# Memory attention in head pairs, a moved transpose group in the first mixer, and head sums by token quarters in the second

## The chip, the cores and the metric

The program runs on one core of one Trainium2 chip. The metric is the device time of one execution in microseconds; lower is better. The figure of a kernel is the median of its runs.

The core's engines run side by side and meet through semaphores: TensorE (PE in the profile; PEld is its weight load), VectorE (DVE), ScalarE (ACT), GpSimd (POOL) and SyncE (SP), which issues the DMAs of the weights.

## The reference, cut to what matters

The sequence has 256 tokens of width 1024, in float32. A first block has two layers; each is a mixer, an attention over 256 memory rows with four heads, an output product, and a SwiGLU network. The mixer of layer 0 is a sparse attention, that of layer 1 an RWKV-7 recurrence. A second block (a gated MLP, a forgetting attention and another SwiGLU network) follows. The change touches the mixers and their memory attention:

```
def _mem_attention(q_mem, mem_n, w_kv):                  # in both layers
    k, v = jnp.split(mem_n @ w_kv, 2, axis=-1)           # 4 heads of 64
    s = jnp.einsum('bshd,bmhd->bhsm', q, k) * (HEAD_DIM ** -0.5)
    p = jax.nn.softmax(s, axis=-1)
    return jnp.einsum('bhsm,bmhd->bshd', p, v).reshape(B, S, MEM_WIDTH)

def _rwkv7_mixer(...):                                   # layer 1: 12 heads of 64
    z, q_mem = proj[..., :RW_SHIFT], proj[..., RW_SHIFT:]
    z = z + (z_prev - z) * mu                            # shift by one token
    r, k, v, zw, za, zg = _split(z, ...)
    w_log = -jax.nn.softplus(-(w0 + jnp.tanh(zw) @ w2)) - 0.5
    decay = jnp.exp(-jnp.exp(w_log))
    a = jax.nn.sigmoid(a0 + za @ a2)
    g = jax.nn.sigmoid(zg) @ g2
    kk = (k * k_k).reshape(B, S, H, N)
    kk = kk / jnp.maximum(jnp.sqrt(jnp.sum(kk * kk, -1)), 1e-12)    # key norms
    k = k * (1 + (a - 1) * k_a)
    y = _wkv7_scan(rh, wh, kh, vh, -kk, kk * ah)
    y = (y - mean) * lax.rsqrt(var + GN_EPS)             # by head, output norm
    bonus = jnp.sum(rh * kh * r_k, -1) * vh
    return (y * lnx_w + lnx_b + bonus) * g, q_mem

x = x + jnp.concatenate([mix, cross], axis=-1) @ w_o[i]
```

In the sparse attention, queries attend to compressed blocks of keys (a softmax over 15 blocks per head), to selected blocks and to a window; the compressed part's probabilities are transposed before they meet the compressed values.

## The kernel before, in words

**Weights and units.** SP loads weights slot by slot into a ring in SBUF. Each product is done as three products of rounded parts (lines 864 to 866, `product`): ScalarE rounds a slot to its high part (line 1823, `split_to`; `high_memory` for the memory units), VectorE subtracts to the low part (line 2363). A unit is one named piece of the projection, as a rule 256 output columns, 48 matmuls of 128x256. `unit()` (line 391) hands out the PSUM bank of each unit ahead of time. `ahead(name)` on ScalarE and VectorE does the split of a unit before it is used. `evac` copies a finished unit out of its bank. Matmuls that aren't split (the small ones of the mixers) are plain float32, each one row of the trace for one of its passes: a form that is issued once shows as two rows.

**Order.** Every engine has an order of its own, written out by hand as Python calls; a semaphore wait in front of an instruction holds all that follows it on that engine. Nothing is planned at run time.

**First mixer.** `sparse_attention` (line 1494) is a loop of 14 steps over pairs of heads. In step s TensorE does the scores of pair s, the transposes of pair s-1 (`pair_turn`), the first fill of that step (`FILLS[s][0]`, half a unit of the projections or of the memory keys and values), the values of pair s-1 and the other fills. `compressed_turns` (line 1409) transposes the compressed probabilities that VectorE has normalized (line 2633), at the end of step 8; ScalarE copies the result out (units pct0 and pct1) in its own step 8. `SPLIT_EARLY` and `SPLIT_BEHIND` say in which step the memory units' halves are split, ahead of or behind the softmax work of the step. `step_end` (line 1969 on ScalarE, 2646 on VectorE) holds the evacuations; that of vmem1 is ScalarE's, in step 13.

**Second mixer.** TensorE's order is z9, z10, qm1, z3, decay, z4, z5, gate, and then `attention("mem1", z_with_memory)`. `decay_and_rate` (line 1552) is 24 rows on 64 partitions for decay and in-context rate; `out_gate` (line 1565) is 24 rows on 128 partitions and twelve rows on the last 32. `attention` (line 1135) takes the four memory heads one at a time: scores of head n, then `z_with_memory(n)`, then the transposes of head n-1 and the values of head n-2. The z units are z0, z1, z2, z6, z7, z8 (keys, then receptance). Between them stand the key norms: `head_sums` (line 1533) adds the squares of the keys over each head's 64 columns, 12 result rows for 256 tokens, behind z0; ScalarE takes the root, VectorE (`prepare`, line 2754) the reciprocal; `head_spread` (line 1542) brings the 12 rows back over 128 partitions, behind z2, from 12 partitions of `head_back`. The sums of the bonus come behind z7. The keys times rw_k_k (kk) are VectorE's, their squares ScalarE's (line 2112), as are two of the exponentials of the decay sums; ScalarE's splits of the next z units stand between them. `late_mix` on VectorE shifts a z unit by one token, and `prepare(step)` does the products that the recurrence needs. The attention's result, token-major, is transposed in `cross_turn` inside `wkv` and joins the operand of the output product wo1.

**Recurrence and output norm.** `wkv` (line 1177) starts with idle products (line 851, products that no one reads) and a wait for `wkv_ready`. After it the variance of each head is summed by `head_sums("gv", ...)`, ScalarE takes the root, VectorE the reciprocal (line 2931), and `head_spread("gr", narrow)` spreads it; wo1 follows, first with the attention's rows.

The two lines of TensorE's loop that the change replaces:

```
        attention("mem1", z_with_memory)
        wkv()
```

Of the kernel before, what the change touches and what calls it, by code (L numbers as in the profile page):

```python
# [21 lines left out]
P = 128  # L22
# [24 lines left out]
SLOT = 2048  # L47

# [22 lines left out]
def shape_constants():  # L71
# [40 lines left out]
    parts["head_back"] = (2 * np.arange(NT)[None, :, None] + t[:, None, :] // DH == i[:, :, None]).reshape(P, -1)  # L112
# [23 lines left out]
def build(nc, T, out, ctx):  # L136
# [197 lines left out]
    cross = take(QT * 256).rearrange("p (q c) -> p q c", q=QT)  # L334
# [21 lines left out]
    VEC_DMAS, SMALL_DMAS = len(VEC) + 1, 4  # L356
# [112 lines left out]
    for name, b in (("q0", 0), ("q1", 1), ("ks", 2), ("vs", 0), ("gl", 1), ("glT", 2), ("kc", 1), ("vc", 0), ("q2", 2), ("hid0", 1),  # L469
                    ("kw", 0), ("hid1", 2), ("kcb", 1), ("vcb", 2), ("vw", 0), ("cs0", 1), ("cs1", 2), ("qm0", 0), ("pct0", 2),  # L470
                    ("pct1", 0), ("kmem0", 1), ("oc0", 0), ("oc1", 1), ("vmem0", 2), ("oc2", 0), ("oc3", 1), ("kmem1", 2),
                    ("vmem1", 1)):
        unit(name, 1, proj.get(name), at=b)
# [14 lines left out]
    for j in Z_ORDER:  # L488
# [6 lines left out]
        if j == 3:  # L495
            for i in range(3):
                unit(f"w2_{i}"), unit(f"a2_{i}")
# [5 lines left out]
        if j in (2, 7):  # L503
            for i in range(3):
                unit(f"kb_{i}" if j == 2 else f"bs_{i}")
# [60 lines left out]
    unit("crT", at=2)  # L566
# [139 lines left out]
    heads = [("mem1", i) for i in range(MH)]  # L706
    heads += [("fox", i) for i in range(NFH)]
    STAGES = {"mem1": range(0, 4), "fox": range(4, 12)}

    def head_parts(n):  # L710

        kind, i = heads[n]
        if kind == "mem1":
            k = kmem1[:, :].rearrange("p (g t) -> p g t", g=2)
            v = vmem1[:, :].rearrange("p (q c) -> p q c", q=QT)
            q = qmem[:, :].rearrange("p (g t) -> p g t", g=2)
            r = slice((i % 2) * DH, (i % 2) * DH + DH)
            return q[r, i // 2, :], k[r, i // 2, :], v[:, :, i * DH:(i + 1) * DH], DH, [(0, 0, S), (1, S, S)]
# [52 lines left out]
    def _(sp):  # L771
# [4 lines left out]
        for n, (name, loads) in enumerate(slots):  # L776
# [3 lines left out]
            if name == "f0_in4":  # L780

                sp.wait_ge(*filled("f0_in0"))
                for dst, src in ((head_back[0:H, :], cst_d[0:H, CONSTANTS:]), (rw_wa2[0:DH, :], T["rw_w2"][0]), (rw_wa2[DH:P, :], T["rw_a2"][0]),
                                 (rw_g2[:, 0:MW], T["rw_g2"][0, 0:P]),
                                 (rw_g2[0:32, MW:2 * MW], T["rw_g2"][0, P:P + 32])):
# [55 lines left out]
    def _(pe):  # L841
# [255 lines left out]
        def scores(n):  # L1097
            q, k, _, _, segs = head_parts(n)
            kind, i = heads[n]
            if n >= 2 and n - 2 in stage:  # L1100
                pe.wait_ge(sem("exp_done" if heads[n - 2][0].startswith("mem") else "nmax_ready"), n - 1)
# [31 lines left out]
        stage = ()  # L1133

        def attention(which, between=None):
            nonlocal stage
            stage = STAGES[which]

            lag = 1
            for n in range(stage[0], stage[-1] + lag + 2):  # L1140
                if n in stage:
                    scores(n)
                if between:
                    between(n - stage[0])
                if n - lag in stage:
                    turn(n - lag)
                if n - lag - 1 in stage:
                    values(n - lag - 1)
# [12 lines left out]
        def cross_product(step):  # L1161

            qt, a, half = step // 4, step // 2 % 2, step % 2
            if step == 0:
                pe.wait_ge(*evacuated("crT"))
# [11 lines left out]
        def wkv():  # L1177

            half = [slice(q * CH, (q + 1) * CH) for q in range(2)]

            def cross_turn():

                begin("crT")
                pe.wait_ge(sem("o_read"), MH)
                for a in range(2):
                    for qt in range(QT):
# [1946 lines left out]
```

## Time and profile before

| | us |
|---|---|
| runs shown | 1181.93, 1184.30, 1184.58 |
| median | 1184.3 |
| profiled execution, its own time | 1186.92 |
| profiled execution, span | 1185.1 |
| mean granted TensorE clock | 0.988 of full speed |
| DMA, whole span | 185.36 MB, mean 156 GB/s |

The profile is one execution, recorded instruction by instruction. The span runs from the first instruction to the last; the execution's own time has 1.8 us around it. The granted clock is TensorE's clock as a share of 2.4 GHz; 0.50 is its lower level, 1.2 GHz. Idle time is put down to the instruction that came last before the wait ended. Names like `bank`, `arena`, `ring` are the program's buffers; `128*12 128x256` in a matmul's row is partitions by columns of the weights, then partitions by elements of the moving operand. All times in the rows further down count from the start of the span.

### The profile page before, as it was taken

The numbers are of one execution on the slowest core, as the hardware profiler recorded it, in microseconds if no ns is written. First come the engines' busy times: TensorE is split into PE (matmuls) and PEld (weight loads), VectorE is DVE, ScalarE is ACT, GpSimd is POOL, SyncE is SP. The second block draws the span as 40 slices with busy tenths as digits, with TensorE's granted clock in tenths as the row PEclk, the third lists the DMA queues.
The fourth block names the chain that finished last, engine by engine and source line by source line (L and its number), as shares of the span: only waits on it lengthen the run. The fifth ranks groups of instructions, "written<-read, shape, count | busy, mean of one in ns | idle before, by whom it ended". The sixth has DMA issues, their size and how long they took to land.

```text
span 1185.1 us, 23306 instructions
## 1 busy us (share of the span) xinstructions
PE 1144.8 (97%) x9880; PEld 1059.2 (89%) x9880; DVE 758.5 (64%) x1309; ACT 601.8 (51%) x1028; POOL 32.0 (3%) x46
## 2 busy tenths in 40 slices
PE   6998999999999999999899999999999999999997
PEld 6997878999888879897799998889999998999986
DVE  5567757667547677765677765375755667676644
ACT  5656656454434672443345444365458745454533
POOL 0000000000000100430000000000000000000000
PEclk9999899999999998999899999999999999999999
DMA  9842257676555432002377665546653445676652
GB/s 281 232 143 72 72 147 192 192 204 187 201 189 157 147 107 72 3 4 73 107 218 217 188 200 190 191 127 203 194 178 112 139 143 142 185 204 183 208 182 71
DMA packets 219053, 185.36 MB, mean 156 GB/s; under 512 B 11404, under 2 KB 204186, under 8 KB 218822
## 3 DMA queue, kind: packets, MB, share of 16 engines
q1 hardware_dynamic: 217370, 181.50, 51.2%
q8 instruction: 78, 1.28, 0.4%
q0 software_dynamic: 384, 1.05, 0.4%
q10 hardware_dynamic: 1196, 1.34, 0.4%
q14 instruction: 25, 0.20, 0.1%
HBM read 181.77 MB, written 1.05 MB: 154 GB/s over the span
## 4 chain that ended last, share of the span: by engine, by line
PE 84%; DVE 9%; ACT 3%; issue 1%; DMA 1%; SPq 0%; DVEq 0%; ACTq 0%
PE bank L864 23%; PE bank L865 23%; PE bank L866 23%; DVE w_lo L2363 2%; PE bank L851 1%; ACT w_hi L1823 1%; PE bank L1241 1%; PE bank L1252 1%; DMA ring<-in_w_ffn_in 1%; DVE act_pair L2345 1%; PE bank L1103 1%; ACT sbuf_p L1940 1%; PE bank L1443 1%; PE bank L1451 1%; PE bank L1129 1%
## 5 line engine op out<-in xcount | busy, mean ns | idle before, releaser
L2363 DVE TENSOR_TENSOR w_lo<-ring,w_hi 128x1024 fp32r<-128x1024 f32 (+2 forms) x332 | 380.5, 1187 | 226.4 <-ACT w_hi L1823 225.4
L1823 ACT ACTIVATE w_hi<-ring 128x1024 fp32r<-128x1024 f32 (+2 forms) x316 | 310.0, 1031 | 381.3 <-PE bank L866 367.0
L864 PE MATMUL bank<-act_pair,w_hi 128*128 128x256 f32 (+1 forms) x1499 | 419.4, 280 | 5.9 <-issue 3.4
L865 PE MATMUL bank<-act_pair,w_hi 128*128 128x256 f32 (+1 forms) x1499 | 415.7, 277 | 0.0
L866 PE MATMUL bank<-act_pair,w_lo 128*128 128x256 f32 (+1 forms) x1499 | 415.6, 277 | 0.0
L864 PEld LDWEIGHTS bank<-act_pair,w_hi 128*128 128x128 f32 (+1 forms) x1499 | 281.4, 188 | 10.0 <-issue 7.4
L865 PEld LDWEIGHTS bank<-act_pair,w_hi 128*128 128x128 f32 (+1 forms) x1499 | 281.3, 188 | 0.3
L866 PEld LDWEIGHTS bank<-act_pair,w_lo 128*128 128x128 f32 (+1 forms) x1499 | 281.0, 187 | 0.3
L864 PE MATMUL bank<-w_hi,act_pair 128*128 128x256 f32 (+1 forms) x436 | 135.6, 311 | 4.9 <-DVE act_pair L2926 1.8
L866 PE MATMUL bank<-w_hi,act_pair 128*128 128x256 f32 (+1 forms) x436 | 133.2, 305 | 0.0
L865 PE MATMUL bank<-w_lo,act_pair 128*128 128x256 f32 (+1 forms) x436 | 133.1, 305 | 0.0
L864 PE MATMUL bank<-w_hi,hT_hi 128*128 128x512 f32 x264 | 102.8, 390 | 1.0 <-DVE w_lo L2363 1.0
L866 PE MATMUL bank<-w_hi,hT_lo 128*128 128x512 f32 x264 | 102.8, 389 | 0.0
L865 PE MATMUL bank<-w_lo,hT_hi 128*128 128x512 f32 x264 | 102.7, 389 | 0.0
L864 PEld LDWEIGHTS bank<-w_hi,act_pair 128*128 128x128 f32 x436 | 82.5, 189 | 11.8 <-issue 4.7
L2492 DVE TENSOR_TENSOR zshift<-bank,row_scale 128x512 f32<-128x512 f32 x66 | 45.6, 691 | 66.5 <-PE bank L866 66.3
L866 PEld LDWEIGHTS bank<-w_hi,act_pair 128*128 128x128 f32 x436 | 82.4, 189 | 4.1
L865 PEld LDWEIGHTS bank<-w_lo,act_pair 128*128 128x128 f32 x436 | 82.5, 189 | 3.8 <-issue 0.2
L864 PEld LDWEIGHTS bank<-w_hi,hT_hi 128*128 128x128 f32 x264 | 49.6, 188 | 11.6 <-issue 1.4
L866 PEld LDWEIGHTS bank<-w_hi,hT_lo 128*128 128x128 f32 x264 | 49.6, 188 | 10.3
L865 PEld LDWEIGHTS bank<-w_lo,hT_hi 128*128 128x128 f32 x264 | 49.6, 188 | 10.1
L1839 ACT ACTIVATE arena<-bank 128x256 f32<-128x256 f32 (+3 forms) x60 | 26.1, 455 | 28.5 <-PE bank L1241 15.6
(339 smaller groups left out, 1274.6 us busy)
## 6 DMA issues: line engine op xcount, KB each, us to landing
ring<-in_w_ffn_in SPq DMA_DIRECT2D x88, 512.0 KB, 5.2
ring<-in_w_in SPq DMA_DIRECT2D x28, 1024.0 KB, 5.2
ring<-in_w_ffn_out SPq DMA_DIRECT2D x22, 1024.0 KB, 4.8
ring<-in_rw_w_in SPq DMA_DIRECT2D x11, 1024.0 KB, 5.3
ring<-in_w_gate SPq DMA_DIRECT2D x22, 512.0 KB, 3.9
ring<-in_w_up SPq DMA_DIRECT2D x22, 512.0 KB, 5.2
ring<-in_w_down SPq DMA_DIRECT2D x11, 1024.0 KB, 4.8
ring<-in_nsa_w_in SPq DMA_DIRECT2D x7, 1024.0 KB, 6.7
```

What stands on the lines that cost most here:

```text
L851: pe.matmul(o[:, 0:P], ident, ident, start=True, stop=True)
L864: pe.matmul(o, ahl[0], bhl[0], start=first, stop=False)
L865: pe.matmul(o, ahl[0], bhl[1], start=False, stop=False)
L866: return pe.matmul(o, ahl[1], bhl[0], start=False, stop=final)
L1103: ins = pe.matmul(score_bank(n)[:, c:c + nk], q[:, qt * P:(qt + 1) * P], k[:, 0:nk], start=True, stop=(kind != "fox"))
L1129: ins = pe.matmul(o_bank(n)[:, o:o + w], sbuf_pt[:, (n % 2) * 512 + c:(n % 2) * 512 + c + P], v[:, kt, :], start=(m == 0), stop=(m == len( ...
L1241: ins = pe.matmul(bank_of(name)[half[q], a * CH:(a + 1) * CH], cms[(len(MERGES) * pr + li) % 2][gi][half[q], a, :], tms[gi][half[q], a, :] ...
L1252: ins = pe.matmul(bank_of(name)[half[q], a * CH:(a + 1) * CH], ems[gi][half[q], a, :], tt[pr][half[q], 4 * gi + a, :], start=True, stop=True)
L1823: ins = act.activation(tiles[0], raw, copy)
L1839: act.activation(dst, bank_of(name)[:, :] if src is None else src, func, scale=scale).then_inc(freed(own, name), 1)
L2363: ins = dve.tensor_tensor(tiles[1], raw, tiles[0], ALU.subtract)
L2492: dve.tensor_tensor(scaled[:, j % 2, :].rearrange("p (b t) -> p b t", b=2), two(f"{tag}_in{j}"), scaled_pair(), ALU.mult).then_inc(freed(o ...
```

## The change

Four groups of edits.

**First mixer.** `compressed_turns` moves from the end of step 8 to step 9, behind the first fill of that step (the second half of kmem0); ScalarE's evacuations of pct0 and pct1 move to step 9, behind that of kmem0, and the unit kmem0 gets its bank ahead of pct0. The split of vmem1's second half moves from the early place of step 12 to behind step 11. The evacuation of vmem1 moves from ScalarE to VectorE.

**Memory attention of layer 1.** Two heads at a time, on the two halves of the partitions: `memory_scores(m)`, `memory_turn(m)`, `memory_values(m)` on TensorE with banks 4 to 7; `memory_exps` and `memory_copy` on ScalarE; `memory_maxima`, `memory_scale`, `memory_finish` on VectorE. The probabilities are scaled before the transposes; the values come out feature-major, so that `cross_turn` and its bank go. z4 moves ahead of `decay_and_rate`, whose rows on the lower and the upper 64 partitions now alternate. The last 32 rows of the gate are laid on three groups of 32 partitions: `rw_g2`'s tail comes with three DMAs for one, and ScalarE writes the sigmoid three times.

**Head sums.** `head_sums` takes the tokens in four quarters, each to its own group of 32 partitions: 24 matmuls of 64 columns for six of 256. `head_sel` grows from 12 to 32 columns a tile (72 to 192 columns), `tok_mask` (256 columns) joins the constants, and `head_back` is stored on 128 partitions for 12. `key_spread`, in the middle of z6, spreads the key norms from the four groups. The output norm's reciprocal is laid out with `tok_mask` in `zdelta` and spread with all 128 partitions.

**ScalarE's and VectorE's order.** ScalarE squares the raw keys with the factor rw_k_k as the scale, takes the three exponentials behind z0, writes kk behind z1 (before: VectorE) and the bonus factor behind z6. VectorE does `prepare` of steps 3 and 5 ahead of the shift of that step, and its products move by a step.

```diff
@@ constants
-    parts["head_sel"] = (heads_of == np.arange(H)[None, None, :]).reshape(P, -1)
+    parts["head_sel"] = (heads_of == np.arange(GROUP)[None, None, :]).reshape(P, -1)
+    parts["tok_mask"] = i // GROUP == np.arange(S)[None, :] // TOK
...
@@ first mixer
-                   9: [("vmem0", 1)], 10: [("kmem1", 0)], 11: [("vmem1", 0)], 12: [("vmem1", 1)]}
+                   9: [("vmem0", 1)], 10: [("kmem1", 0)], 11: [("vmem1", 0)]}
...
-                    10: [("kmem1", 1)]}
+                    10: [("kmem1", 1)], 11: [("vmem1", 1)]}
...
-            if s == 8:
-                compressed_turns()
...
                 fill(*FILLS[s][0])
+                if s == 9:
+                    compressed_turns()
...
@@ TensorE, second mixer
+        def memory_scores(m):
...
+            for qt in range(QT):
+                for p in range(2):
+                    rows = slice(p * DH, (p + 1) * DH)
+                    ins = pe.matmul(bank[4 + p][:, qt * S:(qt + 1) * S], qmem[rows, m * S + qt * P:m * S + (qt + 1) * P],
+                                    kmem1[rows, m * S:(m + 1) * S], start=True, stop=True)
+            ins.then_inc(sem("mem_scored"), 1)
+
+        def memory_turn(m):
...
+            if m:
+                pe.wait_ge(sem("mem_copied"), 2)
+            for p in range(2):
+                pe.wait_ge(sem("mem_scaled"), 2 * m + p + 1)
+                for c in range(0, 2 * S, P):
+                    ins = pe.transpose(bank[6 + p][:, c:c + P], mem_p[m][:, p * 512 + c:p * 512 + c + P], ident)
+                ins.then_inc(sem("mem_turned"), 1)
+
+        def memory_values(m):
...
+            pe.wait_ge(sem("mem_copied"), 2 * m + 2)
+            pe.wait_ge(sem("mem_exp"), 4)
+            for kt in range(QT):
+                for p in range(2):
...
+                    ins = pe.matmul(o, mem_v[:, kt, h * DH:(h + 1) * DH], turned[:, kt], start=(kt == 0), stop=(kt == QT - 1))
+            ins.then_inc(sem("mem_valued"), 1)
...
@@ head_sums
-                ins = pe.matmul(bank_of(name)[0:H, 0:S], C("head_sel")[:, i * H:(i + 1) * H], src[:, i, :],
-                                start=(i == 0), stop=(i == NT - 1))
+                for g in range(GROUPS):
+                    ins = pe.matmul(bank_of(name)[g * GROUP:(g + 1) * GROUP, 0:TOK], C("head_sel")[:, i * GROUP:(i + 1) * GROUP],
+                                    src[:, i, g * TOK:(g + 1) * TOK], start=(i == 0), stop=(i == NT - 1))
...
+        def key_spread(src):
...
+            for i in range(NT):
+                for g in range(GROUPS):
+                    rows = slice(g * GROUP, (g + 1) * GROUP)
+                    ins = pe.matmul(bank_of(f"kb_{g}")[:, i * TOK:(i + 1) * TOK], head_back[rows, i * P:(i + 1) * P],
+                                    src[rows, 0:TOK], start=True, stop=True)
...
@@ out_gate
-                ins = pe.matmul(bank_of(f"g2_{i // 2}")[:, i % 2 * S:(i % 2 + 1) * S], rw_g2[0:32, MW + i * P:MW + (i + 1) * P],
-                                lora[0:32, 2, :], start=False, stop=(i % 2 == 1))
...
+            for a in range(2):
+                for c in range(3):
+                    i, rows = 2 * c + a, slice(c * GROUP, (c + 1) * GROUP)
+                    ins = pe.matmul(bank_of(f"g2_{c}")[:, a * S:(a + 1) * S], rw_g2[rows, MW + i * P:MW + (i + 1) * P],
+                                    lora[rows, 2, :], start=False, stop=(a == 1))
...
@@ TensorE, order
+            if step == 3:
+                fm_unit(LATE_Z[step], fm_of["z"], 0)
+                pe.wait_ge(sem("knorm_ready"), 1)
+                pe.wait_ge(sem("cross_ready"), 1)
+                key_spread(knorm)
+                fm_unit(LATE_Z[step], fm_of["z"], 1)
...
-            if step == 4:
+            if step == 5:
                 bonus_sums()
...
-        attention("mem1", z_with_memory)
+        for step in range(len(LATE_Z)):
+            if step < 2:
+                memory_scores(step)
+            z_with_memory(step)
+            if step in (2, 3):
+                memory_values(step - 2)
+            if step in (1, 2):
+                memory_turn(step - 1)
...
-        head_spread("gr", narrow)
+        head_spread("gr", zdelta[:, S:2 * S])
...
@@ ScalarE
             if step == 0:
-                evac("kn", knorm[0:H, :], ACT.Sqrt, src=bank_of("kn")[0:H, 0:S])
+                act.wait_ge(sem("csum_ready"), 1)
+                act.activation(flat(e_in), flat(csum), ACT.Exp, scale=-C0).then_inc(tick(own, "exps_ready"), 1)
+                act.activation(flat(e_neg), flat(csum), ACT.Exp, scale=C0).then_inc(tick(own, "exps_ready"), 1)
+                act.wait_ge(sem("cexc_ready"), 1)
+                act.activation(flat(sg), flat(sg), ACT.Exp, scale=-C0).then_inc(tick(own, "exps_ready"), 1)
+                act.wait_ge(sem("exps_ready"), 3)
+                evac("kn", knorm[:, 0:TOK], ACT.Sqrt, src=bank_of("kn")[:, 0:TOK])
...
+            if step == 1:
+                for i in range(NT):
+                    ins = act.activation(kk[:, i, :], kraw[:, i, :], copy, scale=V("rw_k_k", i))
...
+        act.wait_ge(sem("zmix_ready"), EARLY_Z)
+        for i in range(NT):
+            ins = act.activation(kk_sq[:, i, :], kraw[:, i, :], ACT.Square, scale=V("rw_k_k", i))
+        ins.then_inc(tick(own, "sumsrc_ready"), 1)
+        for step in range(len(LATE_Z)):
+            if step < 2:
+                memory_exps(step)
+            z_with_memory(step)
+            if step in (1, 2):
+                memory_copy(step - 1)
...
@@ VectorE
+        for step in range(len(LATE_Z)):
+            if step < 2:
+                memory_maxima(step)
+            if step in (3, 5):
+                prepare(step)
+            late_mix(step)
+            if step < 2:
+                memory_scale(step)
+            if step in (2, 3):
+                memory_finish(step - 2)
+            if step not in (3, 5):
+                prepare(step)
...
+        dve.tensor_tensor(zdelta[:, S:2 * S].rearrange("p (g t) -> p g t", g=GROUPS),
+                          narrow[:, 0:TOK].unsqueeze(1).to_broadcast((P, GROUPS, TOK)),
+                          C("tok_mask").rearrange("p (g t) -> p g t", g=GROUPS), ALU.mult).then_inc(tick(own, "rstd_ready"), 1)
```

## Rows read from the trace of the kernel before

**Rows 1.** Part 1 of the page, TensorE, VectorE, ScalarE: busy us, share, instructions

```profile
PE 1144.8 (97%) x9880; PEld 1059.2 (89%) x9880; DVE 758.5 (64%) x1309; ACT 601.8 (51%) x1028; POOL 32.0 (3%) x46
```

**Rows 2.** Busy time by stretch; columns: stretch, length, engines, granted clock, DMA share, GB/s

```profile
110.00:131.00 21.00, 17.76 (x131) 14.94 (x130) 12.98 (x52) 12.42 (x36) 0.00 (x0) 0.84 0.35 100
412.00:440.00 28.00, 25.45 (x175) 20.54 (x173) 18.64 (x27) 21.37 (x35) 2.12 (x1) 0.94 0.31 94
```

**Rows 3.** Waits of TensorE, whole span: total us, times, longest us

```profile
PE bank L1415 <- DVE arena L2633: 3.2, 1, 3.2
PE bank L1538 <- ACT arena L2112: 2.5, 1, 2.5
```

**Rows 4.** Busy time by stretch: four with a low clock, one (456.9) without

```profile
118.60:124.80 6.20, 6.20 (x29) 5.22 (x30) 4.76 (x18) 4.67 (x14) 0.00 (x0) 0.50 0.00 0
421.80:426.10 4.30, 4.28 (x12) 1.38 (x12) 1.16 (x2) 4.30 (x8) 0.00 (x0) 0.61 0.00 0
447.90:455.60 7.70, 7.70 (x49) 7.68 (x49) 3.73 (x9) 1.02 (x4) 0.00 (x0) 0.70 0.14 56
456.90:462.40 5.50, 5.50 (x50) 5.50 (x50) 5.36 (x8) 2.27 (x5) 0.00 (x0) 1.00 0.29 100
569.90:575.40 5.50, 5.50 (x13) 4.34 (x14) 4.79 (x6) 0.63 (x1) 0.00 (x0) 0.50 0.00 0
```

**Rows 5.** The chain that ended last, in order of time: start us, us, what

```profile
99.13 2.78 PE bank L1404 x48
...
171.09 1.01 PE bank L1473 x8
...
426.22 1.06 PE bank L1103 x4
...
440.09 3.26 PE bank L1548 x12
...
472.35 0.84 PE bank L1129 x8
473.19 3.63 PE bank L851 x32
...
489.08 1.43 PE bank L1229 x47
...
563.46 1.75 DVE zdelta L2931
```

**Rows 6.** TensorE by form: rows, columns, out form, count | busy us, mean ns | idle before

```profile
L1538 PE MATMUL bank<-arena,cst 128*12 128x256 f32 x12 | 2.8, 380 | 0.0
...
L1561 PE MATMUL bank<-arena 64*128 64x256 f32 x24 | 3.9, 395 | 1.0 <-issue 0.5 <-ACT arena L2102 0.5
...
L1573 PE MATMUL bank<-arena 32*128 32x256 f32 x12 | 2.9, 383 | 0.0
```

**Rows 7.** TensorE in order of time, the first mixer's last scores: start, us

```profile
145.50 1.13 PE L1443 MATMUL bank<-arena,qmem 64*128 64x256 f32 x8
```

**Rows 8.** ScalarE in order of time, second mixer: start us, us [idle before]

```profile
420.20 1.48 ACT L2112 ACTIVATE arena<-arena 128x1536 f32<-128x1536 f32 x1 [3.37 <-DVE arena L2805]
...
423.86 1.99 ACT L1823 ACTIVATE w_hi<-ring 128x1024 fp32r<-128x1024 f32 x2
425.75 0.90 ACT L2072 ACTIVATE zdelta<-zshift,small 128x256 f32<-128x256 f32 x2
426.67 1.28 ACT L1839 ACT_TABLE_LOAD   x1
...
428.25 3.05 ACT L2084 ACTIVATE arena<-arena,small,vec 128x256 f32<-128x256 f32 x6
```

**Rows 9.** VectorE in order of time, second mixer

```profile
424.94 2.36 DVE L2363 TENSOR_TENSOR w_lo<-ring,w_hi 128x1024 fp32r<-128x1024 f32 x2 [3.45 <-ACT w_hi L1823]
...
437.79 1.76 DVE L2763 TENSOR_TENSOR arena<-arena 128x1536 f32<-128x1536 f32 x1
```

**Rows 10.** DMA issues of the first 48 us: KB each, us to landing

```profile
cst<-shape_constants ACTq DMA_DIRECT2D x1, 1075.0 KB, 6.6
```

More of the change, by code:

```diff
@@ L333, in build @@
     lora = take(3 * S).rearrange("p (i t) -> p i t", i=3)
-    cross = take(QT * 256).rearrange("p (q c) -> p q c", q=QT)
+    cross = take(2 * S).rearrange("p (m t) -> p m t", m=2)
     knorm = take(S)
@@ L502, in build @@
             unit("kn")
-        if j in (2, 7):
+        if j == 2:
+            b = uses["z2"][0][0]
+            for g, at in enumerate(((b + 2) % 4, (b + 3) % 4, b, 4)):
+                unit(f"kb_{g}", at=at)
+        if j == 8:
             for i in range(3):
-                unit(f"kb_{i}" if j == 2 else f"bs_{i}")
+                unit(f"bs_{i}")
     EARLY_Z, LATE_Z = 5, ["z0", "z1", "z2", "z6", "z7", "z8"]
@@ L703, in build @@
     hid_base = {"f0": 0, "f1": FT, "f2": 2 * FT}
[L706 to L708 removed]
+    heads = [("fox", i) for i in range(NFH)]
+    STAGES = {"fox": range(0, NFH)}
+    mem_p = [sbuf_p, sbuf_s]
+    mem_v = vmem1.rearrange("p (q c) -> p q c", q=QT)
+    mem_o = [bank[4 + m][:, 0:S] for m in range(2)]
     def head_parts(n):
         kind, i = heads[n]
[L713 to L718, printed above, removed]
         return q2[:, i, :], k2[:, i, :], v_a[:, :, i * P:(i + 1) * P], P, [(0, 0, P), (1, P, S)]
@@ L1131, in values @@
             ins.then_inc(sem("o_full"), 1)
[L1133 to L1148, printed above, removed]
+        def memory_scores(m):
+            if m:
+                pe.wait_ge(sem("mem_exp"), 2)
+            else:
+                for name in ("w2_1", "a2_1", "w2_2", "a2_2"):
+                    pe.wait_ge(*evacuated(name))
+            for qt in range(QT):
[5 more added lines that the diff above has]
+        def memory_turn(m):
+            if m:
+                pe.wait_ge(sem("mem_copied"), 2)
[9 more added lines that the diff above has]
+                for p in range(2):
+                    h = 2 * m + p
+                    o = mem_o[m][p * DH:(p + 1) * DH, :].rearrange("p (q t) -> p q t", q=QT)
+                    turned = sbuf_pt[:, p * 512:(p + 1) * 512].rearrange("p (q k t) -> p k q t", q=QT, k=QT)
+                    ins = pe.matmul(o, mem_v[:, kt, h * DH:(h + 1) * DH], turned[:, kt], start=(kt == 0), stop=(kt == QT - 1))
+            ins.then_inc(sem("mem_valued"), 1)
         def ffn(tag):
@@ L1861, in copy_pt, with memory_exps, memory_copy @@
             act.activation(sbuf_pt[:, (n % 2) * 512:(n % 2) * 512 + w], pt_bank[:, 0:w], copy).then_inc(tick(own, "pt_copied"), 1)
-        def attention(which, between=None, to_end=False):
-            st = STAGES[which]
-            for n in range(st[0], st[-1] + (3 if to_end else 2)):
-                if n in st:
-                    exps(n)
-                if to_end:
-                    between(n - st[0])
-                if n - 1 in st:
-                    copy_pt(n - 1)
-                if between and not to_end and n in st:
-                    between(n - st[0])
+        def memory_exps(m):
+            act.wait_ge(sem("mem_nmax"), m + 1)
+            for p in range(2):
+                h = 2 * m + p
+                for qt in range(QT):
+                    c = qt * S
+                    ins = act.activation(mem_p[m][:, p * 512 + c:p * 512 + c + S], bank[4 + p][:, c:c + S], ACT.Exp,
+                                         bias=nmax[:, h, qt:qt + 1], accum_out=rsum[:, h, qt:qt + 1])
+                ins.then_inc(tick(own, "mem_exp"), 1)
+        def memory_copy(m):
+            if m:
+                act.wait_ge(sem("mem_valued"), m)
+            for p in range(2):
+                act.wait_ge(sem("mem_turned"), 2 * m + p + 1)
+                act.activation(sbuf_pt[:, p * 512:(p + 1) * 512], bank[6 + p][:, :], copy).then_inc(tick(own, "mem_copied"), 1)
         def high_hidden(tag, j):
@@ L2085, in z_with_memory @@
                 ins.then_inc(tick(own, "rate_ready"), 1)
+            if step == 1:
+                for i in range(NT):
+                    ins = act.activation(kk[:, i, :], kraw[:, i, :], copy, scale=V("rw_k_k", i))
+                ins.then_inc(tick(own, "kk_ready"), 1)
+            if step == 3:
+                act.wait_ge(*filled("kn"))
+                act.wait_ge(sem("zmix_ready"), EARLY_Z + 3)
+                for i in range(NT):
+                    ins = act.activation(bonus[:, i, :], r_fm[:, i, :], copy, scale=V("rw_r_k", i))
+                ins.then_inc(tick(own, "bonus_part"), 1)
             if step == 5:
```

180 lines of the change are left out of this document (83 added, 97 removed).

## The prediction, made before the change was timed

> **What bounds the kernel now.** First the busy shares [rows 1]: TensorE has work in 97% of the span, VectorE in 64%, ScalarE in 51%. So a change pays only where TensorE waits, does work that can go, or runs at its lower clock. Next the stretches with the granted clock [rows 2]: 110 to 131 us (0.84) and 412 to 440 us (0.94) are the places, in the first and the second mixer. The waits [rows 3] name what TensorE stood for: the compressed probabilities of VectorE (3.2 us, once) and ScalarE's squares for the key norms (2.5 us, once; 2.7 counted to the next matmul's start). Last the stretches below full clock [rows 4]: after each of these two waits, and also from 442 and 568.5 us on, where no long wait stands ahead; there the engine had just done twelve matmuls on 12 rows, the head spreads. At the lower level a 48-product unit takes 7.7 us for 5.5 [rows 4]. The lost time is thus waits plus slow clock, and ScalarE's queue, 21.4 of 28 us busy from 412 to 440 [rows 2], is what the change loads further.
>
> **First mixer.** The transposes of the compressed probabilities go from the end of step 8 to step 9, behind half a unit of 24 products. VectorE has the probabilities ready at 118.5 us; before, TensorE stood still from 115.3. In the new order it does scores, turn and half of kmem0 first (0.9 + 0.6 + 2.8 us and 0.4 us for the turn's operand) and reaches the transposes at about 120: no wait. Gone are 3.2 us [rows 3] and the slow stretch behind it, 6.2 us at half speed, 3.1 us lost [rows 4]. What is late next: the copies of the transposed probabilities now stand on ScalarE behind step 9's exponentials, done 0.3 us after TensorE wants them; one softmax in step 12 is late by 1 us because vmem1's second split goes ahead of it, which ends a wait of 1 us on that split. VectorE and ScalarE have 13.0 and 12.4 us of work in 21 us [rows 2], so they can follow a stretch 6 us shorter. VectorE's copy of vmem1 takes its place beside wo0's weights and is free before TensorE comes. Sum: -6.0 (from -3.2, if the clock falls all the same, to -6.5).
>
> **Second mixer, work of TensorE.** Scores: a head alone takes 1.06 us for 4 rows, a pair on two row halves 1.06 for 8 [rows 5, 7]; four heads 4.2 -> 2.1: -2.1. Values: four times 0.84 become two times 1.01 [rows 5]: -1.3. Turns: 8 transposes cost some 0.85, the four of the cross turn go: -0.6. Decay: 24 rows, 3.6 us without their waits, at the pair's 0.133 us a row 3.2: -0.4; the waits around them, 1.4 us (1.0 as idle) [rows 6], go since z4's 5.6 us stand ahead: -1.4. Gate: twelve 32-row matmuls, 2.8 us [rows 6], now three at a time, 0.09 us a row by the pair's price: 1.1, -1.7. Key norms: 12 rows of 256 columns, 2.7 us without the slow clock (2.8 with the tail) [rows 6], become 48 rows of 64 on four column groups; the nearest row are the 64x64 tiles, 0.03 us each [rows 5]: 1.5, -1.2. Their wait goes (-2.7: the squares read the keys themselves, done 2.7 us before TensorE comes), and with it the slow clock, 4.3 us for 2.7: -1.6 [rows 4, 6]. Key spread: 48 rows of 64 columns on four row groups, each with 128 columns of weights; nearest is the 64-row form with 15 columns, where the weights set the pace, 0.056 us [rows 5]: 2.7, as much as the old one at full clock (2.6 of its 3.26 [rows 5]): 0. Bounds: the three new forms from half of this to 0.11 us a row (one after another), that is -3 to +9 us in all, gv's included.
>
> Of the key spread the Trainium skill speaks against a gain (TensorE: Matmul & The Clock Gate, "LDWEIGHTS"): a load costs by its columns, not its rows, and a 32x128 load as much as a 128x128 one. By its formula 128 columns would take 107 ns, an estimate that gives 5.1 us for the 48 and a sum 2.4 us worse; the trace has 56 ns a pair of load and matmul [rows 5], so the rule's direction holds and its size does not, and the row is used.
>
> Slow clock from 442 us: key spread 0.6, turn, values and scores 4.55 us for 2.35 (between the ends of the rows of 440.09 and the start at 447.9), the next unit 2.2 [rows 4, 5]: -5.0, if 128 used rows in place of 12 hold the clock, which is open.
>
> **What it adds there.** ScalarE takes over work: the exponentials of the decay sums now lie behind z0, the product with rw_k_k and the bonus product come to it. The paired values wait for both copies of the transposed weights, and behind step 1 ScalarE has done, counted from the gate's end: three evacuations 1.5, six squares 2.4, table 1.3, four exponentials 1.8, weights 1.9, kept z 0.8, three long exponentials 4.2, table and root 1.6, rate 3.0, table 1.3, four exponentials 1.8, weights 1.9, kept z 0.8, six products 2.4, two copies 1.1: 27.8 us (256 columns 0.40 to 0.49, 1536 columns 1.4, a table 1.29, weights 0.95 a half [rows 8]; evacuations and copies taken as 0.5 by the nearest of them). TensorE has in the same time: scores 1.06, z0 5.6, norms 1.5, scores 1.06, z1 5.6, turn 0.85, z2 5.6: 21.3. So it waits 6.5 us at the first pair's values: +6.5 (4 to 9). Behind values stand turn 1 and z6 on TensorE; z6's weights are split 3 us before ScalarE's copies end, so nothing else is late. After the two waits of 3.5 and 2.7 us before, the clock stayed low for 3.4 to 6.3 us of resumed work [rows 4]; here values and turn double (1.9 us) and half of z6's first half (1.4): +3.3.
>
> From the key spread's end VectorE needs 15.7 us to the bonus products: four products 2.0, two 1536-column operations 3.5, z6's shift, z8's weights and mix 3.9, a copy 0.4, z7's 2.5, two operations 3.4 (1.76 each, weights 2.36 [rows 9]). TensorE has 15.0: half of z6 2.8, values 1.0, z7 and z8 11.2. So the bonus sums wait +0.7 (-0 to +4); the last products end 3.6 us later, under sums 2.6 and idle products 3.63 [rows 5]. Those idle products ran before too, so recurrence start moves as the sum says: -2.1 - 1.3 - 0.6 - 0.4 - 1.4 - 1.7 - 1.2 - 2.7 - 1.6 - 5.0 + 6.5 + 3.3 + 0.7 = **-7.5**.
>
> **Output norm.** The variance sums go 2.7 -> 1.5 [rows 6]; the reciprocal on 256 columns 1.75 [rows 5] becomes one on 64, 0.55 by columns, and a masked product of some 0.4 joins: root to spread is shorter by 0.8, TensorE reaches the spread 1.8 us earlier, idle products filling the rest: -1.8 (0 to -2.5). The spread keeps 12 rows of 256 columns, now on 128 partitions; its time stays. The 12-row form was what ran before the clock fell at 568.5 us, and 5.5 us of products ran at half [rows 4]: -2.7 if the full form holds it. The 1.9 us of idle behind the spread stay; no idle as short cost the clock elsewhere.
>
> **Rest.** 376 more constant columns, 188 KB on a load of 1075 KB that took 6.6 us [rows 10], sit in the first loads: up to 1.2, and half of it taken, since other loads share that time: +0.6 (0 to 1.2). The spread-back constants (348 KB more, two more issues) load during the first FFN, whose weights come ahead of their use: 0; without that cover 2.1 by the same rate.
>
> **Sum.** -6.0 - 7.5 - 1.8 - 2.7 + 0.6 = -17.4 us on the profiled execution's 1186.9: 1169.5. The median shown is 2.6 us lower than that execution, so 1184.3 - 17.4 = **1167 us**.
>
> **Rivals.** (1) *The clock falls again* at the key spread and the last spread, as 32-row tiles or masked rows count no more than 12 rows did. For it: the fall at 442 without any idle. Against it: four tiles at once fill the array. Price: 2.7 back, and 3.9 of the 5.0: 1174. (2) *The first mixer stays as slow*: the copies behind ScalarE's exponentials become the new wait. Against: they end 0.3 us late by the count. 1173. (3) *No wait at the values*, because ScalarE's small operations overlap more than I count: 9.8 us come back, but VectorE's products are then late by 3: 1160. (4) *Slower*: the small tiles cost what a narrow matmul costs. Place: 48 rows each of key norms, key spread, variance sums. A 12-column matmul paid the price of a full one, 0.216 us a row [rows 6]; so priced, 144 rows take 31 us, not 5.7: +25, 1192. It decides above some 0.16 us a row. Against it: 64x64 tiles at 0.03 [rows 5]. The Trainium skill (TensorEngine Tiling (Array Packing), "Key Properties") says that a change of the tiling mode drains the engine; the trace has 32- and 64-row forms between full ones with no idle over 0.5 us, so by that rule a few tenths would be added.
>
> **How the numbers follow.** Forecast 50%, own range 1162 to 1172; rivals 1 to 4: 20%, 10%, 11%, 9%. The range runs from 1159 (no wait) to 1179 (rival 1 with small tiles one after another). About 0.3%, 3.6 us, is what a measurement tells from no change. Faster: all but rival 4 and what two losses together make, 86%; same 5%; slower 9%.
>
> **What would show it.** Right: no low clock between 110 and 130 us; no wait ahead of the key norms; one wait of 4 to 9 us of TensorE, ended by ScalarE's copy, ahead of the first pair's values, and a low clock behind it; 48 rows of norms in 1.5 us, of key spread in 2.7; full clock at the output rows. Wrong: small tiles over 0.1 us a row, a low clock through z6 to z8, or the same 3 us wait in the first mixer.

## The result, and the profile after

The changed kernel takes 1175.35 us (median of five runs, 1174.62 to 1178.89) against 1184.3: a ratio of 0.9927, 95% interval 0.9913 to 0.9941. It is faster, as forecast, but by 8.9 us for 17.3: half of the gain is missing. The time lies above the forecast's own range (1162 to 1172), inside the wide one (1159 to 1179). One of the runs of a variant below (e6) took 6369.78 us and is left out of its ratio.

The profiled execution took 1175.67 us (span 1173.8, granted clock 0.994). Its busy shares, from part 1 of the page, hardly differ from [rows 1]:

```profile
PE 1127.5 (96%) x9968; PEld 1047.9 (89%) x9968; DVE 758.2 (65%) x1303; ACT 608.1 (52%) x1046; POOL 32.0 (3%) x46
```

TensorE lost 17.3 us of busy time, and the span only 11.3. The waits of TensorE over the span (total us, times, longest) say why. Both waits of [rows 3] are gone; these stand in their place:

```profile
PE bank L1170 <- ACT sbuf_pt L1919: 5.7, 1, 5.7
...
PE bank L868 <- ACT arena L1878: 3.1, 1, 3.1
PE bank L1147 <- ACT sbuf_p L1909: 2.3, 1, 2.3
```

The first is the wait forecast at the first pair's values. The second is in the first mixer, 3.1 us, where 3.2 us were to go. The third, ahead of the second pair's scores, was not forecast.

The same two stretches as in [rows 2] (the second moved 7 us forward, with the work), then the stretches behind the new waits, the halves of z6, a unit, and the first output rows, as in [rows 4]; columns as there:

```profile
110.00:131.00 21.00, 17.50 (x144) 14.90 (x144) 13.88 (x56) 11.96 (x36) 0.00 (x0) 0.92 0.36 100
125.40:128.40 3.00, 2.94 (x14) 2.95 (x15) 0.93 (x4) 1.97 (x6) 0.00 (x0) 0.50 0.98 223
405.00:433.00 28.00, 25.42 (x237) 23.00 (x237) 16.57 (x25) 23.57 (x45) 3.44 (x1) 0.94 0.25 76
438.90:442.50 3.60, 3.52 (x17) 2.39 (x17) 3.57 (x4) 3.23 (x6) 0.00 (x0) 0.51 0.47 190
442.50:446.90 4.40, 4.40 (x75) 4.21 (x73) 1.97 (x4) 0.80 (x2) 0.00 (x0) 1.00 0.55 177
451.00:456.60 5.60, 5.60 (x50) 5.60 (x51) 5.57 (x7) 4.32 (x10) 0.00 (x0) 1.00 0.07 8
559.60:565.10 5.50, 5.48 (x24) 4.51 (x25) 4.82 (x6) 0.66 (x2) 0.00 (x0) 1.00 0.01 3
```

The clock is low behind the wait in the first mixer (125.4) and behind the one at the values (438.9), and full through z6 to z8 and at the output rows, where it was 0.50 before. The 0.94 from 405 to 433 us is a low clock behind the third wait, 0.50 to 0.52 from 419 to 422 us, where the second pair's scores take 1.97 us in place of 1.06:

```profile
418.40 1.97 PE L1147 MATMUL bank<-kmem,qmem 64*128 64x256 f32 x8 [2.28 <-ACT sbuf_p L1909]
```

The rows of the new forms, from the chain that ended last (start us, us, what), to be held against [rows 5, 6]:

```profile
438.98 1.98 PE bank L1170 x8
440.96 1.76 PE bank L1158 x8
445.46 1.58 PE bank L1562 x48
551.99 0.81 PE bank L1551 x48
```

L1170 is the values and L1158 the turn, both at half clock; L1562 the key spread; L1551 the variance sums in the new form, 48 rows in 0.81 us, which took 2.7 us as 12 rows of 256 columns.

The sum, part by part, on the two profiled executions (starts of TensorE's rows in each trace; a part ends where the next begins; the last ends with TensorE's last product):

| part | forecast | measured |
|---|---|---|
| start, to the second unit | +0.6 | +0.8 |
| first mixer, to the output product | -6.0 | -1.6 |
| second mixer, to the recurrence | -7.5 | -6.9 |
| recurrence and output norm, to the residual | -7.2 + 2.7 = -4.5 | -5.0 |
| the rest | 0 | +1.5 |
| sum | -17.4 | -11.2 |

### The profile page after: what moved, and what is told of

Read it like the earlier page. It is cut to its first block, busy times and chain, and to the rows that moved or that the text cites. A ratio compares the mean times of both kernels' runs of the same rounds, so it can differ in the third digit from the quotient of the medians.

```text
span 1173.8 us, 23488 instructions
## 1 busy us (share of the span) xinstructions
PE 1127.5 (96%) x9968; PEld 1047.9 (89%) x9968; DVE 758.2 (65%) x1303; ACT 608.1 (52%) x1046; POOL 32.0 (3%) x46
## 4 chain that ended last, share of the span: by engine, by line
PE 79%; DVE 10%; ACT 6%; DMA 2%; issue 2%; SPq 1%; DVEq 0%; ACTq 0%
PE bank L868 22%; PE bank L870 22%; PE bank L869 22%; DVE w_lo L2427 3%; ACT sbuf_p L1986 1%; PE bank L855 1%; PE bank L1254 1%; PE bank L1265 1%; DMA ring<-in_w_ffn_in 1%; ACT w_hi L1862 1%; DMA ring<-in_nsa_w_in 1%; SPq L800 1%; DVE act_pair L2409 1%; PE bank L1067 1%; PE bank L1384 1%
## 5 line engine op out<-in xcount | busy, mean ns | idle before, releaser
L869 PEld LDWEIGHTS bank<-w_lo,hT_hi 128*128 128x128 f32 x264 | 49.6, 188 | 10.1
```

What stands on the lines that cost most here:

```text
L869: pe.matmul(o, ahl[0], bhl[1], start=False, stop=False)
```

## The experiments

Each kernel ran in five rounds beside the kernel before (the second trace of before in one); its ratio to it has an interval of 0.0013 to 0.0018 to either side, 1.6 to 2.1 us. e1 to e4 ran on one chip, e0 and e5 to e7 on another, so a variant is set against the changed kernel by their two ratios (0.9924 in e0); such a difference is uncertain by some 2.2 us. "The stretch" below is from the end of the gate to the first token rows of the recurrence, read in one trace: 64.2 us in the kernel before (62.7 in its second trace, b0), 60.8 in the changed one, and 61.1 to 62.2 in four more traces of the same second mixer.

**The changed kernel again** (e0).

> The changed kernel once more, beside the variants and the kernel before. Theory: the same ratio to before as in the first result, 0.993 (0.991 to 0.994). If the first mixer's edits brought 1.6 us, this one is 0.1% faster than the variant with the first mixer of before, whose ratio was 0.992; if they brought 6, 0.5%.

Measured: 0.9924 (0.9910 to 0.9937), as in the first result.

**The first mixer of before, the rest as changed** (e1).

```diff
-                   9: [("vmem0", 1)], 10: [("kmem1", 0)], 11: [("vmem1", 0)]}
+                   9: [("vmem0", 1)], 10: [("kmem1", 0)], 11: [("vmem1", 0)], 12: [("vmem1", 1)]}
...
+            if s == 8:
+                compressed_turns()
...
-                if s == 9:
-                    compressed_turns()
```

(and the copies, the banks' order and vmem1's copy as before)

> The changed kernel with the first mixer's order of before (compressed transposes at the end of step 8, their copies in ScalarE's step 8, vmem1's split and copy as before); second mixer and output norm as changed. Theory: the first mixer's edits brought only the 1.6 us that the two traces show between the first product and the output product, because the wait for the compressed probabilities turned into a wait for ScalarE's copies; so this one is 1.6 us slower than the changed kernel, about 1177. Rival: they brought the 6.0 us of the forecast and the time was lost elsewhere; then about 1181.

Measured: 0.9923 (0.9910 to 0.9937), the changed kernel in e0 0.9924. The edits of the first mixer brought nothing that can be measured: the rival's 1181 is out, and the theory's 1.6 us is within the uncertainty, neither shown nor excluded. In the traces, from kmem0's first product to the second half of vmem0, this kernel needs 20.7 us, the changed one 19.9. Its wait stands where it was:

```profile
PE bank L1427 <- DVE arena L2703: 2.7, 1, 2.7
```

**The copy of pct0 ahead of the exponentials** (e2).

```diff
+            if s == 9:
+                evac("pct0", p_cmpT[:, 0, :], src=bank_of("pct0")[:, 0:R * P])
             pair_exps(s)
...
                 evac("kmem0", kmem0)
-                for qt in range(QT):
-                    evac(f"pct{qt}", p_cmpT[:, qt, :], src=bank_of(f"pct{qt}")[:, 0:R * P])
+                evac("pct1", p_cmpT[:, 1, :], src=bank_of("pct1")[:, 0:R * P])
```

> The changed kernel with one copy moved: ScalarE copies the first half of the transposed compressed probabilities (pct0) ahead of step 9's exponentials; the copies of pct1 and kmem0 stay behind them. Theory: vmem0's first product waits for nothing but its PSUM bank, which pct0 holds; so the wait of 3.1 us goes, and with it the 1.4 us that the half unit behind it takes longer at the lower clock: -4.5 us, about 1171. Rival: the same time is lost a little later, since the values of step 9 need the copy of pct1, or step 10's softmax comes late: within 1 us of the changed kernel, 1174 to 1175. Second rival: the wait goes and the lower clock stays: -3.1.

Measured: 0.9884 (0.9870 to 0.9897), 4.7 us below the changed kernel, and 4.9 below e1 by the medians of the same chip (1172.22 and 1177.10): that is what the first mixer's edits bring once this copy is out of the way. ScalarE's rows in order of time (start, us, and the idle time before with what ended it), first of the changed kernel:

```profile
122.69 0.40 ACT L1986 ACTIVATE sbuf_p<-sbuf_s,small 128x128 f32<-128x128 f32 x1 [2.99 <-DVE small L2617]
...
124.45 1.32 ACT L1878 ACTIVATE arena<-bank 128x512 f32<-128x512 f32 x3
```

then of this one, in an execution that runs 2 us later here:

```profile
123.36 0.49 ACT L1878 ACTIVATE arena<-bank 128x384 f32<-128x384 f32 x1 [1.73 <-PE bank L1427]
124.62 0.40 ACT L1986 ACTIVATE sbuf_p<-sbuf_s,small 128x128 f32<-128x128 f32 x1 [0.77 <-DVE small L2618]
...
126.39 0.95 ACT L1878 ACTIVATE arena<-bank 128x512 f32<-128x512 f32 x2
```

ScalarE had been idle for 3 us ahead of its exponentials; one copy of 0.5 us fits there, and the exponentials wait for VectorE as before. TensorE's only wait from 115 to 130 us in this kernel:

```profile
PE bank L868 <- DVE w_lo L2443: 0.2, 1, 0.2
```

The wait was for the bank that pct0 held, and the clock stays up without it: from kmem0's first product to the second half of vmem0 it takes 15.3 us in place of 19.9.

**GpSimd's subtraction later** (e3).

```diff
         pool.wait_ge(sem("csum_ready"), 1)
+        pool.wait_ge(sem("zmix_ready"), EARLY_Z)
         pool.tensor_tensor(sg, csum, sg, ALU.subtract).then_inc(tick(own, "cexc_ready"), 1)
```

> The changed kernel with GpSimd's one subtraction of 128x1536 (the exclusive decay sums) held until VectorE has shifted z5. Theory: VectorE's split of z0's weights took 4.0 us in place of 1.2 because GpSimd's subtraction ran beside it; then the split takes 1.2, z5's shift, the squares of the keys and the first pair's exponentials come 2.8 us earlier, the wait of 2.3 us ahead of the second scores goes, and since ScalarE's queue still sets the first pair's values, the total is -2.8 us, about 1172.5. Rival: the split was long for another reason (its weights, its buffer): it stays at 4 us and the time does not change. Second rival: the subtraction only meets VectorE's next operations and stops those: 0 to -1 us.

Measured: 0.9883 (0.9869 to 0.9896), 4.9 us below the changed kernel; the stretch is 58.1 us for 60.8 to 62.2. The theory's 2.8 is at the edge of the uncertainty; it had left out the low clock behind the second scores' wait, which goes too (1.00 from 405 to 433 us here, 0.94 and 0.88 in the two traces of the changed kernel). VectorE and GpSimd in the changed kernel, in order of time; the VectorE row holds both halves of z0's split, one of 4.0 and one of 1.2 us:

```profile
405.75 5.16 DVE L2427 TENSOR_TENSOR w_lo<-ring,w_hi 128x1024 fp32r<-128x1024 f32 x2
410.95 0.69 DVE L2810 TENSOR_TENSOR zdelta<-zshift 128x512 f32<-128x512 f32 x1
```

```profile
405.26 3.44 POOL L830 TENSOR_TENSOR arena<-arena 128x1536 f32<-128x1536 f32 x1 [338.00 <-DVE arena L2870]
```

and in this kernel:

```profile
405.93 2.36 DVE L2428 TENSOR_TENSOR w_lo<-ring,w_hi 128x1024 fp32r<-128x1024 f32 x2
408.33 0.69 DVE L2811 TENSOR_TENSOR zdelta<-zshift 128x512 f32<-128x512 f32 x1
```

```profile
410.09 3.52 POOL L831 TENSOR_TENSOR arena<-arena 128x1536 f32<-128x1536 f32 x1 [343.67 <-DVE arena L2816]
```

The split is back at 2.4 us, and all that hangs on it is 2.8 us earlier, counted from the gate's end: z5's shift, ScalarE's squares (from 4.4 to 1.6) and the first pair's copies (end 28.0 for 30.8). The wait ahead of the second scores is gone; of TensorE's waits from 405 to 445 us one is left, longer, since TensorE comes earlier:

```profile
PE bank L1171 <- ACT sbuf_pt L1920: 7.2, 1, 7.2
```

The Trainium skill (SBUF — State Buffer, "SBUF: two separate sides") says that GpSimd and a VectorE operation with two SBUF inputs take a shared port by turns, for a whole instruction each; the trace agrees, 4.0 us for a split of 1.2 that met a GpSimd operation of 3.4: it ends 1.1 us after GpSimd's. In the kernel before the two did not meet: VectorE's split of z0's weights waited for ScalarE's until just after GpSimd was done, as VectorE's and GpSimd's rows show:

```profile
414.45 2.36 DVE L2363 TENSOR_TENSOR w_lo<-ring,w_hi 128x1024 fp32r<-128x1024 f32 x2 [3.29 <-ACT w_hi L1823]
```

```profile
410.67 3.46 POOL L826 TENSOR_TENSOR arena<-arena 128x1536 f32<-128x1536 f32 x1 [344.29 <-DVE arena L2801]
```

Two long exponentials stood ahead of that split on ScalarE. The change moved them behind z0, and so set the split free to meet GpSimd.

**The two copies ahead of the products kk** (e4).

```diff
             if step == 1:
+                memory_copy(0)
                 for i in range(NT):
                     ins = act.activation(kk[:, i, :], kraw[:, i, :], copy, scale=V("rw_k_k", i))
...
-            if step in (1, 2):
+            if step == 2:
                 memory_copy(step - 1)
```

> The changed kernel with ScalarE's two copies of the first pair's transposed weights ahead of the six products with rw_k_k, not behind them. Theory: the wait of 5.7 us at the first pair's values is ScalarE's queue, so it falls by the six products, 2.4 us, to 3.3, and VectorE, which needs these products only behind the key spread, is not late: -2.4 us, about 1173. Rival: the wait becomes shorter, but the second pair's turn then waits for VectorE's scaling, which ended at 438.6, or the bonus sums wait longer: 0 to -1 us.

Measured: 0.9916 (0.9902 to 0.9929), 1.0 us below the changed kernel, inside the uncertainty. The copies end 28.4 us behind the gate for 30.8, as the queue's count says, and TensorE's wait is shorter by as much:

```profile
PE bank L1170 <- ACT sbuf_pt L1919: 3.3, 1, 3.3
```

The stretch is 60.0 us for 60.8 to 62.2. So ScalarE's queue is what TensorE waits for there; that the 2.4 us come through in full is not shown.

**All three** (e5: the diffs of e2, e3 and e4).

> The changed kernel with the three repairs at once: the copy of pct0 ahead, GpSimd's subtraction behind z5's shift, the first pair's two copies ahead of the products with rw_k_k. Theory: they sit at three places and add up, -4.5, -2.8 and -2.4: 9.7 us less than the changed kernel, ratio to before about 0.985. Rival: ahead of the key spread VectorE takes ScalarE's place as the last to be ready, and half of the third is lost: 8.5 less.

Measured: 0.9867 (0.9850 to 0.9885), 6.8 us below the changed kernel; its runs spread from 1167.0 to 1171.8. That is less than the theory's 9.7; the rival's 8.5 is within the uncertainty. Its trace has both gains (15.9 us for 19.9 in the first mixer, 57.4 for 60.8 to 62.2 in the stretch) and a wait at the values of 4.8 us. Whether the missing 3 us are lost in the other executions or never come can't be told from one trace.

**The last spread on 12 partitions** (e6).

```diff
-                                    head_back[:, i * P:(i + 1) * P], src, start=True, stop=True)
+                                    head_back[0:H, i * P:(i + 1) * P], src[0:H], start=True, stop=True)
```

> The changed kernel with the last head spread (before the output product) on 12 partitions of both operands in place of 128; same number of matmuls, columns and waits; it leaves out the scale of three quarters of the tokens, so only its time counts. Theory: twelve matmuls on 12 partitions let the clock fall, as at 568.5 us in the kernel before, and 5.5 us of products behind them run at half: +2.7 us. Rival: the idle stretches around it made the clock fall; then the full clock stays and the time does not change.

Measured: 0.9941 (0.9926 to 0.9956), 2.0 us above the changed kernel. As a time, that is not clear of the uncertainty; the traces decide. From the recurrence's start to the residual its trace has 110.1 us for 107.2; the 5.5 us behind the spread:

```profile
561.40:566.90 5.50, 5.50 (x13) 4.34 (x14) 4.79 (x6) 0.63 (x1) 0.00 (x0) 0.50 0.02 3
```

The idle time around the spread is the same (1.8 us behind it, in both) and the clock falls, as at 569.9 us in [rows 4]. In all three traces with the twelve rows on 12 partitions (two of before, this one) the 5.5 us behind them ran at 0.50, in all eight with 128 partitions at 1.00; so the partitions that the twelve rows use decide it here.

**The exponentials together** (e7: e2 and e3, and)

```diff
                 act.wait_ge(sem("exps_ready"), 3)
+                memory_exps(1)
+                memory_copy(0)
                 evac("kn", knorm[:, 0:TOK], ACT.Sqrt, src=bank_of("kn")[:, 0:TOK])
...
             if step == 0:
                 memory_scale(0)
+                memory_maxima(1)
+                memory_scale(1)
```

(VectorE's copies of the attended values go ahead of that step's shift)

> Two of the three repairs (copy of pct0 ahead, GpSimd's subtraction later), and ScalarE's order changed further: the second pair's exponentials and the first pair's two copies directly behind the exponentials of the decay sums, ahead of the root of the norms and the rate; VectorE takes the second pair's maxima and scaling ahead of the norms' reciprocal. Theory: the first pair's values wait for nothing (the variant with three repairs leaves some 4.3 us there), and VectorE's products behind the key spread set the end instead, so that about half comes through: 2 us less than the three repairs. Rival: all of it comes through, 4 us less. Second rival: VectorE, held at the norms' reciprocal behind ScalarE, is so late that nothing is won.

Measured: 0.9820 (0.9807 to 0.9833), 1163.88 us, 12.3 below the changed kernel and 21 below the kernel before: the fastest of all. It is 5.7 us below e5 by the medians and 3.1 by the two traces: the theory's 2 is too little, and the first rival's 4 lies between the two measures. The stretch takes 53.8 us, and the waits in it are VectorE's now, ahead of the key spread, in z6 and ahead of the bonus sums:

```profile
PE bank L1563 <- DVE zshift L2802: 1.8, 1, 1.8
PE bank L1612 <- DVE arena L2855: 1.5, 1, 1.5
PE bank L869 <- DVE w_lo L2431: 1.3, 1, 1.3
```

The clock stays at 1.00 behind each of them, from 398 to 460 us.

**The kernel before once more** (b0).

> The kernel before once more, for a second trace of it. The prediction's terms were sized on one execution of 1186.9 us, 2.6 above the median. Theory: executions of one kernel differ by short stretches of half clock behind runs of small matmuls (in five of nine traces of the changed kernel and its variants the clock between 99.8 and 109.5 us is 1.00, in the others 0.65 or 0.82), so this trace has the three long waits of the first trace at the same places, and other low-clock stretches, by which its time differs. Rival: the two traces are the same within 0.5 us in each stretch.

Measured: 1183.69 us in its profiled execution, 3.2 less than in the first one (four of the nine traces named there have the full clock, not five). Two of the long waits are shorter: 2.6 us for the compressed probabilities, 0.9 for the squares. And other stretches are slow; the same three in the first trace, then in this one (behind the scores of the compressed attention, behind the compressed wait, at the key norms, which begin 2 us earlier here and take 2.75 us for their 12 rows):

```profile
99.80:109.50 9.70, 9.70 (x105) 8.93 (x105) 7.82 (x35) 6.54 (x20) 0.00 (x0) 1.00 0.32 109
118.00:126.00 8.00, 7.44 (x39) 6.46 (x40) 5.84 (x22) 5.30 (x16) 0.00 (x0) 0.57 0.00 0
421.00:427.00 6.00, 5.18 (x16) 2.05 (x16) 2.55 (x3) 5.98 (x11) 0.00 (x0) 0.72 0.06 18
```

```profile
99.80:109.50 9.70, 9.70 (x90) 8.61 (x89) 6.96 (x32) 6.18 (x19) 0.00 (x0) 0.82 0.32 108
118.00:126.00 8.00, 6.78 (x57) 5.84 (x58) 7.10 (x29) 6.20 (x20) 0.00 (x0) 1.00 0.06 13
421.00:427.00 6.00, 6.00 (x41) 4.58 (x39) 3.67 (x6) 5.97 (x13) 0.00 (x0) 1.00 0.09 11
```

From kmem0's first product to the second half of vmem0 this execution takes 17.9 us, the first one 21.2: less than the changed kernel's 19.9. The low clock behind the two head spreads is in both traces (from 441 to 453 us 0.57 and 0.65). Held against this execution, the parts of the changed kernel come out as +0.6, +0.6, -5.5, -5.3 and +1.5, together -8.1 us, near the medians' 8.9, and the first mixer's edits as no gain, as in e1.

## Why half of the forecast gain did not come

**First mixer: the step that failed.** "The copies of the transposed probabilities now stand on ScalarE behind step 9's exponentials, done 0.3 us after TensorE wants them." They were done 3.1 us after, for two reasons that the order of the code held. ScalarE's exponentials wait for VectorE's maxima (2.99 us idle in the row above), and these stand behind the compressed probabilities and a split of vmem0's weights, so the exponentials began at 122.7, though TensorE's scores had ended at 116.9. VectorE in the changed kernel, the probabilities' last step, the split and the first maximum:

```profile
118.77 0.54 DVE L2701 TENSOR_TENSOR arena<-arena,small 128x360 f32<-128x360 f32 x1
119.22 1.67 DVE L2442 SCALAR_TENSOR_TENSOR w_lo<-ring,vec,w_hi 128x256 fp32r<-128x256 f32 x4
...
121.25 0.29 DVE L2612 CUSTOM_DVE_ANT_0 sbuf_s<-bank,cst 128x128 f32<-128x128 f32 x1
```

And the first to want a copy is vmem0's first product, whose bank is the one that pct0 holds: three banks serve these units, and kmem0, pct0 and pct1 held all three. The part ahead of this held: the transposes began at 120.7 us and waited for nothing. So a wait of 3.2 us became one of 3.1, with 3.0 us at 0.50 behind it for 6.2. That both engines had work for only 13.0 and 12.4 of 21 us could not show this: what counted was the order of their work. Rival 2 named this mechanism (1173 us) and had 10%; its working used the same wrong 0.3. e2 shows the cause: with the one copy moved, this part takes 15.3 us for 21.2, the forecast's 6 (2.6 less than the second trace of before).

**The price of the clock.** The 3.1 us of slow products behind the compressed wait and the 1.6 at the norms were read in one execution, 2.6 us above the median; the second trace of before, 1 us below the median, has neither (e1, with the same first mixer, has the first again: 0.84 from 110 to 131 us). So part of -6.0 and of the norms' terms was not there in every execution, and to subtract the whole sum from the median was wrong: the traces differ by 11.2 us and the medians by 8.9. This accounts for 2.3 of the 8.4 us between forecast and result; the first mixer for 4.4, the rest of the program, which the change doesn't touch, for 1.5 (it takes 590.5 us in both traces of before, 590.9 to 592.1 in those of the changed kernel and its variants, with no wait that explains it; why is open). The range had slips of its own, which don't bear on the forecast: 144 small rows at 0.11 us are 10.1 us dearer than 5.7, not 9, which with rival 1 gives 1184, not 1179; and the unit of 7.7 us "at the lower level" has a mean clock of 0.70 in its row.

**Second mixer: the sum near, by luck.** Errors of both signs cancel in -6.9 for -7.5. Right: the gate (twelve rows in 1.1 us), the decay (2.8 us, no wait), the wait at the values by ScalarE's queue (5.7 for 6.5), the bonus sums' wait (0.7), the full clock through z6 to z8. Too dear: the small tiles. The forecast took 0.03 and 0.056 us a row by the nearest forms; measured are 0.017 for the sums and 0.031 for the key spread, 2 us less in all. The Trainium skill's formula (TensorE: Matmul & The Clock Gate, "LDWEIGHTS") gives 107 ns for a load of 128 columns, an estimate; a row here takes 31 ns, and the measurement decides. The prediction read its 56 ns as the price of a load with its matmul; but that form goes to two groups of 64 partitions in turn, the key spread to four groups of 32, and in both a group gets a load and a matmul every 112 to 125 ns. The loads of different groups overlap: the trace has each of the 48 as 181 to 187 ns long, all in 1.5 us. Rivals 1 and 4 are out. Not seen: GpSimd's subtraction. The queue was counted as 27.8 us from the gate's end; it took 30.8, the 27.8 and an idle stretch of 2.8 ahead of the squares, which e3 traces to that subtraction. So the squares, counted as done 2.7 us early, came 0.3 us late. The subtraction also made the wait of 2.3 us ahead of the second scores, which the count had free by 1 us, and the low clock behind that. The half of z6 at low clock that was charged with 1.4 us ran full in this execution; it came in some of the others.

**Output norm.** -5.0 for -4.5; e6 confirms the reason given for 2.7 of it, the form of the last spread (2.9 us between the two traces). The start cost what was forecast, to 0.2 us.

## What to carry to other kernels

Before you move work ahead of a unit, list who holds its PSUM bank and on which engine, behind what, that bank is emptied: the wait that you remove comes back there. When a queue is shortened, look at what the work set free will now run beside; an operation on another engine that was hidden by a wait is not hidden any more. And price a clock that falls from more than one execution: half of what was to be won in the first mixer was not lost in the second trace of the kernel before.

## What was not expected of the hardware

A matmul of 64 columns on a quarter of the array costs 17 ns a row when the four quarters are used in turn (48 rows in 0.81 us, plain float32), so a sum over heads costs less in 48 such rows than in 12 rows of 256 columns (2.7 us). The clock behind the same run of small matmuls (48 rows of 64x15 from 99.8 us on) was 1.00 in four of nine traces of the changed kernel and its variants and 0.65 or 0.82 in the others, worth up to 3 us. It is one of the things that set executions apart, but not the one that set the two of the kernel before apart: the slower had the full clock there.
